# Expert weights on two issuing queues: the first three pieces of each expert on the sync engine's, the last three on ScalarE's

## What is computed

```python
logits = (hf @ w_router + b_router).astype(f32)
top_val, top_idx = lax.top_k(logits, TOP_K)          # TOP_K = 4 of N_EXPERTS = 32
gate = jax.nn.softmax(top_val, axis=-1)
...
def expert_block(args):
    xb, e = args
    gu = xb @ w_gu[e] + b_gu[e]                       # w_gu[e]: 1024 x 2048
    g, u = gu[:, :D_FF], gu[:, D_FF:]
    g = jnp.minimum(g, SWIGLU_LIMIT)
    u = jnp.clip(u, -SWIGLU_LIMIT, SWIGLU_LIMIT)
    return ((u + 1.0) * (g * jax.nn.sigmoid(SWIGLU_ALPHA * g))) @ w_down[e] + b_down[e]   # w_down[e]: 1024 x 1024
```

## Time and profile before

| | us |
|---|---|
| median of 3 runs (1359.56 to 1366.99) | 1361.69 |
| profiled execution, its own time | 1362.65 |
| profiled execution, span | 1360.9 |
| TensorE busy | 1256.9 (92%) |
| VectorE busy | 281.3 (21%) |
| ScalarE busy | 146.7 (11%) |
| one expert block in mid run | 30.1 |

### The profile page before, as it was taken

One profiled execution on the slowest core, in us unless ns is written; L12 is line 12 of the kernel. 1 busy time (PEld: TensorE's weight loads), 2 busy tenths in 40 slices (PEclk: granted clock), 3 DMA queues, 4 the chain that ended last, 5 costly groups with the idle time before them and its releaser, 6 DMA issues.

```text
span 1360.9 us, 15150 instructions
## 1 busy us (share of the span) xinstructions
PE 1256.9 (92%) x6309; PEld 615.3 (45%) x6309; DVE 281.3 (21%) x686; ACT 146.7 (11%) x328; POOL 11.0 (1%) x38
## 2 busy tenths in 40 slices
PE   6999999899999999999999888899998899998886
PEld 6868886576754343333333333333333333333321
DVE  1143234221122121111211111122111121221111
ACT  2113222101410000000000000000000000000001
POOL 1000000000000000000000000000000000000000
PEclk9999999899999998999999999999999999999999
DMA  9972323336447999999999999999999999999995
GB/s 322 275 246 86 124 71 115 133 131 213 162 189 295 416 417 418 396 415 416 418 418 418 418 418 417 417 417 419 419 419 418 419 416 416 416 417 418 417 418 232
DMA packets 103378, 456.79 MB, mean 336 GB/s; under 512 B 6252, under 2 KB 17064, under 8 KB 70568
## 3 DMA queue, kind: packets, MB, share of 16 engines
q1 hardware_dynamic: 102696, 454.07, 84.4%
q0 software_dynamic: 640, 2.10, 0.4%
HBM read 455.10 MB, written 1.05 MB: 335 GB/s over the span
## 4 chain that ended last, share of the span: by engine, by line
PE 52%; DMA 44%; DVE 1%; ACT 1%; issue 1%; SPq 0%; DVEq 0%
DMA ring<-in_w_gu_dram 44%; PE ps L1195 20%; PE ps L823 14%; PE ps L830 8%; PE ps L1172 1%; PE ps L1188 1%; PE ps L983 1%; PE ps L812 1%; PE ps L1258 1%; PE ps L891 1%; PE ps L1126 0%; PE ps L874 0%; PE ps L1108 0%; DMA r_x<-in_x_dram 0%; PE ps L1279 0%
## 5 line engine op out<-in xcount | busy, mean ns | idle before, releaser
L1195 PE MATMUL ps<-ring,r_memT 128*64 128x512 f32 x1280 | 290.9, 601 | 51.3 <-DMA ring<-in_w_gu_dram 50.6
L1195 PE MATMUL ps<-ring,r_kx 128*64 128x512 f32 x1024 | 226.8, 595 | 0.9 <-DVE r_kx L1841 0.8
L1195 PEld LDWEIGHTS ps<-ring,r_memT 128*64 128x64 f32 x1280 | 89.3, 138 | 247.1 <-issue 157.7
L1829 DVE TENSOR_SCALAR r_ga<-ps 128x512 f32<-128x512 f32 x32 | 22.1, 691 | 705.3 <-PE ps L1195 705.3
L1195 PEld LDWEIGHTS ps<-ring,r_kx 128*64 128x64 f32 x1024 | 72.2, 137 | 154.0 <-issue 143.5
L823 PE MATMUL ps<-r_hT,ring 128*128 128x256 f32 x576 | 130.0, 386 | 0.0
L823 PEld LDWEIGHTS ps<-r_hT,ring 128*128 128x128 f32 x576 | 110.7, 194 | 17.7 <-issue 2.5
L768 ACT ACTIVATE r_ga<-r_ga 128x512 f32<-128x512 f32 x32 | 20.1, 630 | 544.7 <-DVE r_ga L1829 544.7
L1188 PE MATMUL ps<-r_kx,r_dm 64*128 64x512 f32 x256 | 63.6, 615 | 0.7 <-ACT r_kx L772 0.7
L1172 PE MATMUL ps<-r_dm,r_x 128*128 128x128 f32 x512 | 62.3, 275 | 1.7 <-DVE r_dm L1759 1.7
L1172 PEld LDWEIGHTS ps<-r_dm,r_x 128*128 128x128 f32 x512 | 59.6, 192 | 1.7 <-issue 1.7
(11 more groups left out here) (333 smaller groups left out, 917.4 us busy)
## 6 DMA issues: line engine op xcount, KB each, us to landing
ring<-in_w_gu_dram SPq DMA_DIRECT2D x80, 2048.0 KB, 25.9
ring<-in_w_down_dram SPq DMA_DIRECT2D x64, 2048.0 KB, 22.2
ring<-in_w_in_dram SPq DMA_DIRECT2D x8, 2048.0 KB, 12.5
r_at<-in_w_gu_dram SPq DMA_DIRECT2D x16, 1024.0 KB, 25.4
r_xmc<-in_w_gu_dram SPq DMA_DIRECT2D x16, 1024.0 KB, 21.8
r_mem<-in_w_gu_dram SPq DMA_DIRECT2D x16, 1024.0 KB, 18.4
r_tp<-in_w_gu_dram SPq DMA_DIRECT2D x16, 1024.0 KB, 19.6
r_xs<-in_w_gu_dram SPq DMA_DIRECT2D x16, 1024.0 KB, 23.1
```

The source lines that it names most:

```text
L1195: last = mm(ps[n * SLOTS:(n + 1) * SLOTS, bk, :], stationary_, moving(n), start=start, stop=stop, skip_group_check=True)
L1829: V.tensor_scalar(gact, ps[:, GBK, :], 7.0, None, ALU.min).then_inc(g_limited, 1)
```

## The change

`others` leaves the sync engine's list, which keeps the heads of all experts in their order and waits for nothing but the heads' own slots. ScalarE gets a function `load_other`, and `block_steps(i)` issues the others of expert i+1: gu3 behind the sigmoid, dn0 behind the copy of the turned places, dn1 behind the copy of the output. The others of expert 0 stay on the sync engine. What is loaded, where to, what each issue waits for, and all compute instructions are as before.

```diff
-            def others(i):
-
-                for j in range(HEADS, 6):
-                    sp.wait_ge(freed[eslot[EXPERT_PIECES[j]]], i)
-                    expert_piece(i, j)
...
             even_heads(1)
-            others(1)
-            for p in (1, 2):
+            with sp.Fori(1, NE // 2 - 1) as p:
                 odd_heads(p)
-                others(p * 2)
                 even_heads(p + 1)
-                others(p * 2 + 1)
-            with sp.Fori(3, NE // 2 - 1) as p:
-                others(p * 2)
-                odd_heads(p)
-                others(p * 2 + 1)
-                even_heads(p + 1)
-            others(NE - 2)
             odd_heads(NE // 2 - 1)
-            others(NE - 1)
...
+            def load_other(i, j):
+                name = EXPERT_PIECES[j]
+                slot = eslot[name]
+                act.wait_ge(freed[slot], i)
...
+                act.dma_start(dst, src).then_inc(loaded[slot], 16)
+
+            def block_steps(i, more_follow=True):
                 act.wait_ge(g_limited, i + 1)
                 nc.scalar.activation(sig, gact, ACT.Sigmoid, scale=1.702).then_inc(sig_done, 1)
+                if more_follow:
+                    load_other(i + 1, 3)
                 act.wait_ge(pt_done, i + 1)
                 nc.scalar.activation(scat, ps[:, GBK, 0:T], ACT.Copy).then_inc(scat_ready, 1)
+                if more_follow:
+                    load_other(i + 1, 4)
                 act.wait_ge(freed[eslot["dn1"]], i + 1)
                 nc.scalar.activation(y_slot, ps[:, ZBK, :], ACT.Copy).then_inc(yslot_ready, 1)
+                if more_follow:
+                    load_other(i + 1, 5)
```

More of the change, by code:

```diff
@@ L765, in _ @@
             last.then_inc(r_exp, 1)
-            def block_steps(i):
+            def load_other(i, j):
+                name = EXPERT_PIECES[j]
+                slot = eslot[name]
+                act.wait_ge(freed[slot], i)
+                if j < 4:
+                    dst, src = ring[:, slot].rearrange("p (k n) -> p k n", k=2), gu_dram[i, j]
+                else:
+                    dst, src = ring[:, slot].rearrange("p (k n) -> p k n", k=4), dn_dram[i, j - 4]
+                act.dma_start(dst, src).then_inc(loaded[slot], 16)
+            def block_steps(i, more_follow=True):
                 act.wait_ge(g_limited, i + 1)
                 nc.scalar.activation(sig, gact, ACT.Sigmoid, scale=1.702).then_inc(sig_done, 1)
+                if more_follow:
+                    load_other(i + 1, 3)
                 act.wait_ge(pt_done, i + 1)
                 nc.scalar.activation(scat, ps[:, GBK, 0:T], ACT.Copy).then_inc(scat_ready, 1)
+                if more_follow:
+                    load_other(i + 1, 4)
                 act.wait_ge(freed[eslot["dn1"]], i + 1)
                 nc.scalar.activation(y_slot, ps[:, ZBK, :], ACT.Copy).then_inc(yslot_ready, 1)
+                if more_follow:
+                    load_other(i + 1, 5)
             block_steps(0)
-            with act.Fori(1, NE) as i:
+            with act.Fori(1, NE - 1) as i:
                 block_steps(i)
+            block_steps(NE - 1, False)
             drained_of(act, "meta")
@@ L780, in _ @@
                 with act.Fori(NE, nblk) as i:
-                    block_steps(i)
+                    block_steps(i, False)
             square_root_table()
```

## The result

The change is slower: 1383.99 us at the median of 4 runs (1376.71 to 1389.39) against 1363.31 for the kernel before (four runs now; the three that I had gave 1361.69), a ratio of 1.0148 (95% interval 1.0092 to 1.0205). I had predicted 1372 in a range of 1364 to 1382. The direction was right, the size twice what I said (+20.7 us, not +10), and the time lies above the range. The profiled executions are 19.8 us apart in time and in span (1382.42 and 1380.7 against 1362.65 and 1360.9).

A forecast was written before the change was run, and what follows sets the result against it. The prediction took DMA transfers at 418 GB/s as the bound. Terms -1.9 (idle stretch), 0 (issuing) and +11.5 (order of arrival) gave +9.6, rounded to +10 us, so 1372 us, range 1364 to 1382.

The forecast's parts named there:

- What bounds the kernel: Expert blocks: transfers at 418 GB/s set the 30.1 us block; TensorE needs 26.3 us and waits for gu3.
- Bytes and rate: All transfers: bytes and rate unchanged, only an idle stretch between experts' loads goes; -1.9 us, bounds -1.9 and 0.
- the stretch at 574: 574 to 580 us, DMA engines at 288 GB/s because expert 7's heads stood behind others; filling it saves 1.9 us.
- Issuing: ScalarE, three issues per block, 93 in all, about 0.37 us each and covered by other work; term 0.
- the rival of a held ScalarE: ScalarE held 9.4 us by gu3's issue with many pieces outstanding, biases 7.7 us late at the end; 1379, chance 0.13.
- Order of arrival: Lists share equally, TensorE's wait moves to dn1, loss paid once at the end; +11.5 us, bounds +5.1 and +20.2.
- The rival of turns by packet: DMA engines alternate rows, so w_down's 4 KB rows get a third beside 8 KB heads; 1378, chance 0.17.
- r: Heads of expert 31 still to move when TensorE gets dn1 of expert 29; forecast 1.7, loss 20.2 - 5.02 x r.
- The walk: Both lists followed from 418.5 us at equal shares; the heads' lead stays constant from expert 3, r = 1.7.
- The rival of arrival in the order of issue: DMA engines serve both lists in issue order, so r = 3 at the end; +3 us, 1365, chance 0.20.

The follow-up runs named there:

- the runs with 8 and 16 KB: The change with w_down read in rows of 8 KB or 16 KB instead of 4 KB: 1357.43 us and 1356.60 us.
- the split with 8 KB: The change (two lists) with w_down read in rows of 8 KB instead of 4 KB: 1357.43 us, 0.9953 of the kernel before.

## Why the prediction was wrong

- **What bounds the kernel** was right: bytes at 418 GB/s, TensorE with a few us to spare, the order of the one list near the best. What I missed in the earlier trace rows is that the rate itself hangs on the packets: I used them for a rival's share and not for a price. The runs of one list with longer rows show it: 418, 422 and 424 GB/s with 103378, 86994 and 78802 packets.
- **Bytes and rate** (-1.9 us): right in its place, the stretch at 574 runs at 416 GB/s in the change. It assumed that no new idle time comes. That failed: 13.3 us came, in the three holes above, and the last weights are in about 9 us later. The sum had no term for it, since it put T where it was.
- **Issuing** (0): right, 0.38 us each; the rival of a held ScalarE is refuted.
- **Order of arrival** (+11.5 us): that TensorE's wait moves to dn1 of the single buffered list and that the loss is paid at the end was right. The step that failed is the one where I let both lists share equally. The share goes by packet, 0.34 for `w_down` beside the heads, and the runs with 8 and 16 KB turn the picture as that says. With a third of the rate dn1 comes late in about every other block, and the last wait is for dn1 of expert 28, 83 us before the end of `down`, where I had expert 29 and 54 us. The 11.5 us look right against the 11 measured behind the last byte, and so do the 14 us of idle DMA engines at the end against 15, but that is luck: they were worked out for a last wait at expert 29 with r = 1.7, and the trace has it at expert 28, with an r of 2.5 at expert 29. (The term has a slip too: 20.2 - 5.02 x 1.7 is 11.7.)
- **The rival of turns by packet** gave 1378 and a bound of +18; measured is 1384, +20.7 by the medians. Its share was right. Its r = 0 was not: when dn1 of expert 29 lands, at 1307.6, 2.5 heads of expert 31 are still out, since their tiles came free only in block 29; and it too had no term for idle DMA engines. Its chance of 0.17 was too low: the packet sizes stood in the earlier trace rows, and nothing in the trace spoke for equal shares.
- **TensorE's clock** was in no sum. Behind the last wait, one of 6.2 us, the granted clock is 0.50 from 1286 to 1290 (1.2 GHz, the lower of its two levels) and 1.00 again from 1292. In the window 1286 to 1312 behind the last wait the granted clock is 0.89, and 80 matmuls take 19.77 us instead of the 17.4 in the split with 8 KB: 2.4 us. In mid run such losses are nearly hidden behind the transfers: the rate stays at 415 to 419 GB/s but for the slice of 408. I read this and did not try it apart.
- **The walk** for equal shares was wrong too, in the other direction: r grew from 2 to 4, and equal rows cost 3.4 us and not 9.6. Two errors of the same part met, so a time near the forecast would not have proved it.
- **The rival of arrival in the order of issue** is excluded by the change itself: the dn1 issued at 888.29 landed 31.2 us later, while the three heads issued from 891.7 to 898.6 took 11.9 to 21.0, so that the first two landed ahead of it. **The Trainium skill's** sentence, in "DMA: Bandwidth & Descriptors", section "Issuing engines are not separate DMA queues", that several issuers only save issue time, holds for the rate (418 and 417 GB/s) and not for the time. The same page's section "Queues, rings and completion order" has an engine turn between queue rows packet by packet. With the profile's packets, one for each row of a piece, the shares of 0.34, 0.51 and 0.68 agree.

## What to carry to other kernels

Where one list in the order of need keeps the DMA engines full, a second list adds no rate and takes the order away; what is loaded ahead for later is taken from what is needed next, and it is paid where there is no later. Before splitting, compare the rows of both lists: the one with the longer rows gets more. And look at the packet sizes of a transfer-bound kernel first: doubling the rows of a third of the bytes brought 0.7% by three lines.

## What was not expected of the hardware

- A packet has a price beside its bytes, also at 4 and 8 KB. Per expert, 2048 packets took 30.1 us, 1536 took 29.8, 1280 took 29.7; 0.28 us for 512 packets over 16 engines is 9 ns for each packet of an engine. The packets' own durations point the same way: in mid run one of 4 KB took 164 ns on average, one of 8 KB 314 and one of 16 KB 617, so twice the bytes took 11 to 14 ns less than two packets.
- TensorE's granted clock falls behind waits that the kernel before hardly had. Waits of 5.6 us on average (78.4 / 14) in the change bring the granted clock over the span from 0.99 to 0.962; with 8 KB rows, where no wait of the matmuls is over 3.7 us, it is 0.975. The expert part of the kernel before has one wait of 3.3 us and none over 1.6 besides: the granted clock is 0.95 from 506 to 574 us, where the one of 3.3 lies, and 1.00 from 640 to 900, where each block has two of about 1.3.
- An issue can hold its engine while another engine's is free: 4.9 us on the sync engine, 0.4 on ScalarE, in the same microseconds. What depth of a list brings this on was not measured.
